# A four-layer block, a hybrid mixer and an expert gather on one core: first-tile rows in ticks of their own, modulation pieces on TensorE, ring loads behind them

## What is computed

```
cond = silu(c)
for i in range(4):                                   # gla, sgu, fox, gla
    shift, scale, gate = split(cond @ w_mod[i] + b_mod[i], 3)
    h = rms_norm(x, norm_pre_g[i]) * (1 + scale) + shift
    x = x + gate * rms_norm(mixer_i(h), norm_post_g[i])
x = x + hybrid_mixer(rms_norm(x, norm_mix))
u = rms_norm(x, norm_ffn)                            # expert layer
# per token 8 heads x 16 picks = 128 picks out of 16384 experts, by top-k over two key sets
a   = gelu(einsum('cd,ced->ce', u, expert_down[idx]))
x   = x + einsum('ce,ced->cd', softmax(best) * a, expert_up[idx])
out = rms_norm(x, final_norm)
```

## Time and profile before

| quantity | value |
|---|---|
| median of 3 runs (lowest, highest) | 1791.57 us (1786.73, 1792.23) |
| the profiled execution's own time | 1788.6 us |
| its span | 1786.8 us |
| PE busy | 1415.5 us, 79% of the span |
| DVE busy | 1034.1 us, 58% |
| ACT, POOL busy | 439.6 us, 489.7 us |
| moved by DMA | 591.53 MB, 331 GB/s over the span |
| mean granted TensorE clock | 0.897 of full |

### The profile page before, as it was taken

The page is one execution under the profiler, slowest core; times in us unless marked ns, Lnnn a source line. Parts: engine busy times, 40 slices in busy tenths (PEclk is TensorE's granted clock), DMA queues, the critical chain, the costliest instruction groups (busy, mean ns, idle before and its releaser), DMA issues. The chain is left out here.

```text
span 1786.8 us, 13852 instructions
## 1 busy us (share of the span) xinstructions
PE 1415.5 (79%) x4134; PEld 714.8 (40%) x4134; DVE 1034.1 (58%) x2185; ACT 439.6 (25%) x993; POOL 489.7 (27%) x498
## 2 busy tenths in 40 slices
PE   2998978798989999996968667698588676776665
PEld 2444445354444554443534333455233322222222
DVE  6654553653132223116587974997963467887875
ACT  2122313425224321011433131231012212211112
POOL 2101100210000000004236435554452354544441
PEclk8998998989999999998978779698799878888888
DMA  9978985976747777879879979999999699999995
GB/s 387 394 248 307 349 307 189 370 280 220 260 171 277 251 264 256 317 261 346 326 281 395 403 239 409 365 415 415 395 410 381 226 418 402 405 422 421 422 421 218
DMA packets 108941, 591.53 MB, mean 331 GB/s; under 512 B 12450, under 2 KB 12706, under 8 KB 60612
## 3 DMA queue, kind: packets, MB, share of 16 engines
q0 software_dynamic: 67776, 312.56, 44.7%
q1 hardware_dynamic: 41092, 278.10, 41.5%
HBM read 589.55 MB, written 1.05 MB: 331 GB/s over the span
## 5 line engine op out<-in xcount | busy, mean ns | idle before, releaser
L928 PE MATMUL bank<-ring,hT 128*128 128x512 f32 x1888 | 867.6, 615 | 44.1 <-DVE room L2009 12.0
L928 PEld LDWEIGHTS bank<-ring,hT 128*128 128x128 f32 x1888 | 366.2, 198 | 488.2 <-issue 451.1
L1168 PE MATMUL bank<-room 128*128 128x512 f32 x360 | 202.0, 713 | 90.2 <-ACT room L1458 74.6
L1757 DVE CUSTOM_DVE_ANT_0 room<-room 128x1024 f32<-128x1024 f32 x172 | 209.1, 1221 | 93.5 <-DMA room<-in_pair,idx 56.0
L859 POOL DMA_INDIRECT room<-in_peer_down,idx x84 | 91.9, 1094 | 514.8 <-DVE idx L1741 402.1
L1168 PEld LDWEIGHTS bank<-room 128*128 128x128 f32 x360 | 78.0, 228 | 211.1 <-ACT room L1458 110.4
L1772 DVE SCALAR_TENSOR_TENSOR x<-room,pcoef,x 128x1024 f32<-128x1024 f32 x113 | 145.3, 1286 | 27.0 <-DMA room<-in_peer_up,idx 23.6
L859 POOL DMA_INDIRECT room<-in_peer_up,idx x115 | 123.4, 1073 | 133.1 <-PE bank L1168 49.7
L907 PE MATMUL bank<-cst,room 128*128 128x128 f32 x424 | 65.7, 300 | 91.5 <-DVE room L1500 43.0
L859 POOL DMA_INDIRECT room<-in_pair,idx x88 | 100.9, 1147 | 111.6 <-PE bank L1168 51.7
L831 POOL DMA_DIRECT2D room<-in_w_mod x80 | 42.3, 530 | 318.1 <-DVE room L1527 199.8
(11 more groups left out here) (298 smaller groups left out, 1456.5 us busy)
## 6 DMA issues: line engine op xcount, KB each, us to landing
ring<-in_wpk SPq DMA_DIRECT2D x248, 1024.0 KB
room<-in_w_mod POOLq DMA_DIRECT2D x80, 512.0 KB
room<-in_w_mod SPq DMA_DIRECT2D x8, 1024.0 KB, 22.9
room<-in_norm_post_g POOLq DMA_DIRECT2D x4, 512.0 KB, 4.8
rowb<-in_gate_bias SPq DMA_DIRECT2D x4, 512.0 KB
room<-in_peer_up,idx POOLq DMA_INDIRECT x115
room<-in_pair,idx POOLq DMA_INDIRECT x88, 12.8
room<-in_peer_down,idx POOLq DMA_INDIRECT x84
```

Of the source, the lines that this page charges most:

```text
L928: last = mm(bank[p][:, :], lhs, ring[:, h % 4, k * N:(k + 1) * N], start=(kk == 0), stop=(h == halves[-1] and k == 3))
L1168: last = mm(bank[WORK[tile][i]][:, :], diag[:, nth % 4, :], row[:, i * N:(i + 1) * N], start=(v == mine[0]), stop=(v == mine[-1]), skip_gr ...
L1757: v.tensor_tensor_reduce(out=row, in0=row, in1=u_(k // MINE), scale=1.0, scalar=0.0, op0=ALU.mult, op1=ALU.add, accum_out=pa[:, k // TOPK ...
```

## The change

- The first tile's last 18 `up` rows get 18 ticks of their own (`REST`): ticks 128 to 145 issue only an `up` row, and pair g belongs to tick g+18. There are 18 ticks more. POOL no longer waits for head 8 before these rows. The rows may use all places, and the pairs take their places in a fixed round that starts with the fifth place in `room` and the four in `ring`; the places 0 to 3 also wait for the last row of a row place whose semaphore they share.
- `on_vector` gives DVE rows 96 to 111 as well, each odd row of 112 to 127, and each odd one of the last eight rows (248 to 255).
- `spot` counts rows instead of ticks against its limit, so it can place six ticks where a tick is one row.
- Of the first 16 modulation pieces, 5, 7, 9, 11, 13 and 15 are not added by DVE. PE multiplies each directly: eight matmuls with a moving side of one column (`piece_columns`), two pieces ahead of everything else and four right before `mod_cols` of layer 0, whose matmuls add to the same columns.
- The first four ring loads also wait for the sixth early load. POOL's first four fetches wait for the ten pieces that DVE still adds (before: for four). DVE's first piece waits for one bias load instead of three.
- ACT loads the table of exp and ln at `final` before it waits for the sums.

```
@@ -229,50 +229,66 @@
-TICKS = PICKS + LEAD[1]
+REST = LEAD[0]
+TICKS = PICKS + REST + LEAD[1]
...
+PE_PIECES = (5, 7, 9, 11, 13, 15)
+
+
+def summed_before(n):
+    return n - sum(i < n for i in PE_PIECES)
...
 def on_vector(u):
-    return u < 6 * TOPK or u % 4 == 3
+    return u < 7 * TOPK or u % 4 == 3 or (u % 2 and (u < MINE or u >= PICKS - 8))
+
+def tick_of(g):
+    return g if g < MINE else g + REST
+
+
+def pick_of(k):
+    g = k if k < MINE else k - REST
+    return None if MINE <= k < MINE + REST or g >= PICKS else g
...
 def added_at(v):
-    return v + LEAD[v // MINE]
-
-
-BORN = [0] * 9 + [9, 9] + [20, 20]
-PAIR, PAIR_LAST = {}, {}
-_last = {}
-for _g in range(MINE, PICKS):
-    _free = [p for p in range(len(BORN)) if _g - MINE >= BORN[p]]
-    _p = min(_free, key=lambda p: _last.get(p, p - 100))
-    PAIR[_g] = (_p, sum(PAIR[g][0] == _p for g in PAIR))
-    if _p in _last:
-        PAIR_LAST[_g] = _last[_p]
-    _last[_p] = _g
+    return tick_of(v) + LEAD[v // MINE]
+
+
+PLACES = (4, 5, 6, 7, 8, 0, 1, 2, 3, 9, 10, 11, 12)
+PAIR = {g: (PLACES[(g - MINE) % len(PLACES)], (g - MINE) // len(PLACES)) for g in range(MINE, PICKS)}
+PAIR_LAST = {g: g - len(PLACES) for g in range(MINE + len(PLACES), PICKS)}
...
-GROUP_AT = {g + n: i for i, (g, n) in enumerate(GROUPS)}
+GROUP_AT = {tick_of(g + n - 1) + 1: i for i, (g, n) in enumerate(GROUPS)}
@@ -396,10 +412,9 @@
     def spot(most):
         rows.add_due()
-        for _ in range(most):
-            target = start + (stop - start) * gone // whole
-            if asked(rows.at) < target:
-                rows.tick()
+        target, most = start + (stop - start) * gone // whole, asked(rows.at) + 2 * most
+        while asked(rows.at) < min(target, most):
+            rows.tick()
@@ -447,13 +462,12 @@
-for _k in range(MINE + LEAD[0]):
+for _k in range(MINE + REST):
...
-        _free = [s for s in PREFER if BORN_AT.get(s, 0) <= _k and not (s in ROWB and _k >= ROWB_ENDS)
-                 and (_k < MINE - 4 or 4 <= s < 8)]
-        _s = min(_free, key=lambda s: (SLOT_LAST[s][0], PREFER.index(s)) if s in SLOT_LAST else (-1, PREFER.index(s)))
+        _s = min((s for s in PREFER if BORN_AT.get(s, 0) <= _k and not (s in ROWB and _k >= ROWB_ENDS)),
+                 key=lambda s: (SLOT_LAST[s][0] if s in SLOT_LAST else BORN_AT.get(s, 0) - 1, PREFER.index(s)))
@@ -698,6 +712,9 @@
+        def sums_set(L):
+            return 48 * (L // 2 + 1) - (0 if L % 2 else 16)
@@ -808,6 +825,7 @@
                         else:
                             sp.wait_ge(S(early_in(h)), 16)
+                            sp.wait_ge(S(early_in(5)), 16)
                         load(ring[:, h % 4, :], A["wpk"][first + i], f"w_in{h % 4}")
@@ -826,7 +844,7 @@
             def fetch(n):
                 L, third, k = PIECES[n]
-                pool.wait_ge(S("summed"), 4 if n < 2 * KC + 4 else n - 3)
+                pool.wait_ge(S("summed"), summed_before(2 * KC if n < 2 * KC + 4 else n - 3))
@@ -837,7 +855,7 @@
                     pool.dma_start(sums[L % 2][i][0:1, :], A["b_mod"][L:L + 1, i * D:(i + 1) * D]) \
-                        .then_inc(S(f"sums_init{L % 2}"), 16)
+                        .then_inc(S("shift_init" if L == i == 0 else f"sums_init{L % 2}"), 16)
@@ -862,10 +880,10 @@
             for step in ORDER:
                 if step[0] == "tick":
-                    g, v = step[1], step[1] - LEAD[0]
-                    if g % TOPK == 0 and g < PICKS:
+                    g = pick_of(step[1])
+                    if g is not None and g % TOPK == 0:
                         pool.wait_ge(S("picked"), g // TOPK + 1)
-                    for kind, r in (("dn", g), ("up", v)):
+                    for kind, r in (("dn", step[1]), ("up", step[1] - LEAD[0])):
                         if not 0 <= r < MINE:
                             continue
                         i, _ = ROW[kind, r]
...
-                    if MINE <= g < PICKS:
+                    if g is not None and g >= MINE:
                         p, nth = PAIR[g]
                         if g in PAIR_LAST:
                             up_used(pool, PAIR_LAST[g])
                         elif p < 5:
                             pool.wait_ge(S("scm1"), 4)
+                            if p < 4:
+                                row_used(pool, SLOT_LAST[8 + p][1])
                         elif p < 9:
                             n, b = use("mm", 1, "query", 3)
                             pool.wait_ge(S(f"pd{b}"), n // 2 + 1)
@@ -957,9 +977,21 @@
...
+            def piece_columns(n, p):
+                _, third, k = PIECES[n]
+                pe.wait_ge(S(early_in(n // 2)), 16)
+                for j in range(KC):
+                    mm(bank[p][:, third * KC + j:third * KC + j + 1], early[n // 2][:, n % 2, j * P:(j + 1) * P],
+                       const("cond", k, 1), start=n == PE_PIECES[0] and j == 0, stop=False, skip_group_check=True)
...
             pe.wait_ge(S("first_in"), 16)
             pe.wait_ge(S("ones_set"), 1)
             pe.wait_ge(S("pool_order"), 1)
+            pe.wait_ge(S("cond"), 1)
+            for piece in PE_PIECES[:2]:
+                piece_columns(piece, use("mod_cols", 0)[1])
@@ -968,19 +1000,22 @@
-                    pe.wait_ge(S(f"sums_init{L % 2}"), 48 * (L // 2 + 1))
+                    if L == 0:
+                        for piece in PE_PIECES[2:]:
+                            piece_columns(piece, p)
+                    pe.wait_ge(S(f"sums_init{L % 2}"), sums_set(L))
                     for j in range(2 * KC):
                         if j % KC == 0:
-                            pe.wait_ge(S("summed"), L * 3 * KC + j + KC)
+                            pe.wait_ge(S("summed"), summed_before(L * 3 * KC + j + KC))
                         last = mm(bank[p][:, j:j + 1], sums[L % 2][j // KC][:, (j % KC) * P:(j % KC + 1) * P],
-                                  ones[:, 0:1], start=True, stop=True)
+                                  ones[:, 0:1], start=L > 0, stop=True, skip_group_check=L == 0)
@@ -1458,6 +1493,7 @@
                 elif kind == "final":
+                    nc.scalar.preload_act_table_set(EXP_SET)
                     act.wait_ge(S(f"out{t}"), 1)
@@ -1511,12 +1547,16 @@
             def add_piece(n):
                 L, third, k = PIECES[n]
-                if n % (3 * KC) == 0:
-                    dve.wait_ge(S(f"sums_init{L % 2}"), 48 * (L // 2 + 1))
+                if n in PE_PIECES:
+                    return
+                if n == 0:
+                    dve.wait_ge(S("shift_init"), 16)
+                elif n % (3 * KC) == 0 or n == KC:
+                    dve.wait_ge(S(f"sums_init{L % 2}"), sums_set(L))
                 if n == 0:
                     dve.wait_ge(S("cond"), 1)
                 else:
-                    dve.wait_ge(S("summed"), n)
+                    dve.wait_ge(S("summed"), summed_before(n))
@@ -1751,12 +1791,13 @@
             def tick(k):
-                if k < PICKS:
-                    row, landed, count = landed_row("dn", k)
+                g = pick_of(k)
+                if g is not None:
+                    row, landed, count = landed_row("dn", g)
                     dve.wait_ge(landed, count)
...
-                hh, e = k // TOPK, k % TOPK
+                if g is None:
+                    return
+                hh, e = g // TOPK, g % TOPK
                 if hh + 1 < T * PH and hh + 1 != PH and e in (2, 4, 6, 8):
                     choose(hh + 1, e // 2 - 1)
```

More of the change, by code:

```diff
@@ L259 @@
 DVE_NTH = {u: i for i, u in enumerate(ON_DVE)}
+ADDS = {added_at(v): [v] for v in range(PICKS)}
 def adds_of(k):
-    return [v for v in (k - LEAD[0], k - LEAD[1]) if 0 <= v < PICKS and added_at(v) == k]
+    return ADDS.get(k, [])
 def sums_at(hh):
-    return (hh + 1) * TOPK if hh < PH else MINE + 1 if hh == PH else (hh - 1) * TOPK + 6
+    return (hh + 1) * TOPK if hh < PH else MINE + 1 if hh == PH else (hh - 1) * TOPK + REST + 6
 EXP_NTH = {hh: i for i, hh in enumerate(sorted(range(T * PH), key=lambda hh: (sums_at(hh), hh)))}
@@ L322, in tick @@
             self.add_through(v - 4)
-        self.add_through(PAIR_LAST.get(self.at))
+        self.add_through(PAIR_LAST.get(pick_of(self.at)))
         for v in adds_of(self.at):
@@ L326, in tick @@
                 self.add_through(ON_PE[PE_NTH[v] - 4])
-        if self.at == MINE + BORN[-1]:
+        if self.at == tick_of(MINE + 9):
             self.add_through(MINE - 1)
@@ L425, in make_order @@
         rows.add_due()
-        if rows.at == MINE + LEAD[0] + 8:
+        if rows.at == tick_of(MINE + 8):
             rows.add_through(MINE - 1)
@@ L1233, in _ @@
                         if L == 3 and t == 0 and i == 0:
-                            act.wait_ge(S("summed"), len(PIECES))
+                            act.wait_ge(S("summed"), summed_before(len(PIECES)))
                         if L == 3 and t == 0 and i == 2:
@@ L1449, in _ @@
                         w, e = g // TOPK % 4, g % TOPK
```

(11 more changed lines are left out.)

2 lines of the change are left out of this document (1 added, 1 removed).

## The result

| | before | changed |
|---|---|---|
| median of the runs | 1791.9 us (4 runs, 1786.7 to 1792.3) | 1745.1 us (4 runs, 1739.4 to 1747.6) |
| profiled execution | 1788.6 us, span 1786.8 | 1739.4 us, span 1737.6 |
| ratio, with 95% interval | | 0.9739 (0.9714 to 0.9765) |

The change is 46.8 us faster; the forecast had 27, and its range ended at 1749. The prediction was right on the sign and wrong on the size.

The account below looks back on a forecast made before the run. DMA was taken as full except a hole at 1360 to 1415 us, a late start and the tail. From 1788.6: -24 + 0 + 2 - 5 = -27, 1761.6; 3.0 more for the median, 1764.5 us; range 1749 to 1783.

Parts of the forecast that it names:

- Part 1: DMA hole at 1360 to 1415 us: own ticks for rows and 16 more rows on DVE fill it; 24 us gained.
- The bound: Saturated DMA from 1360 us on: 158.0 MB at 0.421 MB/us takes 375 us, it took 405; at most 30 gained.
- the ten rows that were to go out during the picking: While DVE picks head 8, ten rows can still go out: 5.2 MB or 12.5 us of transfers.
- (b): Rival: the hole is filled by half because POOL waits for DVE; 12 us instead of 24, 1776.5; chance 0.15.
- Part 2: Ticks three earlier move up to six rows from 1150 to 1360 into 820 to 1150 us; 0 us.
- Part 3: Start: loads arrive earlier, but modulation columns on PE end at 43.6, 3.5 us late; 2 us lost in all.
- (a): Rival: the clock stays full through the columns, start 2 us gained instead of 2 lost; 1760.5; chance 0.10.
- Part 4: Tail: last rows split anew save 2.4 us, one early table load replacing two saves 2.6; 5 us gained.
- (c): Rival: the earlier ticks lengthen 820 to 1150 us, 7 us lost; 1771.5; chance 0.07.
- (d): Rival: rows in their own ticks become a serial chain, first pair at 1451; slower, 1796; chance 0.04.
- (e): Rival: POOL waits for the scores anyway and the hole only moves; 1788.6; chance 0.04.
- the signs the forecast named: Hole's DMA share 0.9 or more, POOL's PE waits gone, columns done at 43 to 44, one end table load, 17 us tail.

Follow-up runs that it names:

- e10: The changed kernel with both the old rule for ticks and the old preference for row places; 1770.1 us, ratio 0.9894.
- T: The change's new rule for where a tick may go, which puts ticks earlier; alone on the kernel before it measured 1782.1 us.
- P: The change's new preference for row places: a place just come into being waits behind places free for longer; alone on the kernel before 1778.2 us.
- e2: The kernel before with only the new rule for where a tick may go; 1782.1 us, ratio 0.9940.
- e15: The kernel before with only the new preference for row places; 1778.2 us, ratio 0.9928.
- e11: The kernel before with the new rule for ticks and the new preference for row places, nothing else; 1767.1 us, ratio 0.9870.
- e12: The changed kernel run once more, word for word, in a later set; 1742.2 us, ratio 0.9741.
- e6: The changed kernel without the table load ahead of the last normalization; 1750.5 us, ratio 0.9766.
- e9: The changed kernel with ticks moved earlier still, by two (three at the third layer's first blocks); 1752.0 us, ratio 0.9788.
- e7: The changed kernel with three of the first sixteen modulation pieces on PE (5, 7 and 9) instead of six; 1738.6 us, ratio 0.9718.

## Why the prediction was right or wrong

**Part 1, the hole, 24 us: right in mechanism, too large.** e10 is the change without T and P, so it has just the parts that the forecast gave a price other than 0. It gained 19 us where the sum said 27. Its stretches:
```profile
1360.00:1415.00 55.00, 37.04 (x117) 18.93 (x115) 40.14 (x77) 12.79 (x26) 28.11 (x26) 0.84 0.92 357
1415.00:1530.00 115.00, 63.59 (x118) 24.16 (x117) 90.82 (x222) 24.44 (x57) 52.78 (x49) 0.85 1.01 414
```
Over rows 2 that is 5.9 and 1.8 MB more, 7.7 MB, 18 us at 0.421 MB/us. By the time it is 19 less the tail's 4.5, and 1 or 2 more for the start, 15 to 17. So part 1 was worth 15 to 18. Three things were off. The bound took 0.421 MB/us for the hole as well, but at 0.92 of full share the hole moves 357 GB/s, which makes 388 at full share. And the picking of head 8 was put at 1379.5 to 1388.6, behind PE. In e10 PE's last query block ends at 1384.34 (forecast 1386), and ACT has the scores of head 8 ready at 1378.2. But DVE works on three `dn` and three `up` rows without a gap from 1377.87 and comes to the picking only at 1385.52. And the ten rows that were to go out during the picking did not: POOL issues one more at 1386.72 and then waits 8.88 us, the DMA share from 1390 to 1400 is 0.60, and the first pair goes out at 1420.77 and not at 1411. That is part of rival (b).

**Part 2, the ticks three earlier, 0 us: wrong. Here the forecast failed, and in the term that it did not have (next paragraph).** The forecast said that "both stretches pay in the same coin", because DVE is about as busy in each. DVE's share of busy time was the wrong thing to compare. In 820 to 1150 us the DMA share was 0.91 with dips under 0.6, and in the stretch behind it 1.0. A MB moved from the full stretch into a dip was gained, with DVE as busy as it was. The upper bound of 7.5 us was near: 11 us (7 to 14, by the interval of e2) in the kernel before.

**The preference for row places: not in the forecast at all.** It stands in the diff as the key of a `min`, and its price stood in the trace, 11.96 and 19.64 us of POOL's waiting. It is worth 13 us by itself (10 to 16, by the interval of e15). With part 2 this is the whole of what was missing: 23 us (e11), less the 8 by which the rest was set too high, and some 5 more when everything is together (47 - 19 - 23), which the intervals hardly separate from 0.

**Part 3, the start, 2 us lost: near for the columns, its cost at the end not shown.** The forecast gave 43.6 for the modulation columns, between 37.9 and 45.5; they ended at 45.97 in the profiled change, just outside, and at 42.82 in e12. Of PE's lateness at the first projection (5.9 us) 2.4 us were left at 84 us, and the bytes are 2.5 us behind at 87 us, 1.0 in e12 (389 GB/s). Further on it can't be followed. POOL's first gather of a row, at the end of tile 0's chain, is at 815.13 before and 821.25 in the change, but at 820.29 in e2 and 821.87 in e11, which have the old start. No run takes the whole start back. How many pieces PE takes makes no difference that the runs can show. The 2.30 us that the forecast took for a group at full clock are not the least: at the second layer's columns the first group took 1.84 us (144.04, before) with the clock at 1.00. Rival (a) did not come: in e12 the granted clock falls to half while PE is busy without a gap with one-column matmuls.
```profile
26.00:32.00 6.00, 6.00 (x44) 6.00 (x45) 2.57 (x2) 0.00 (x0) 1.25 (x3) 0.81 1.04 428
32.00:39.00 7.00, 7.00 (x34) 7.00 (x35) 0.00 (x0) 0.00 (x0) 0.85 (x2) 0.50 0.99 408
```
The Trainium skill ("TensorE: Matmul & The Clock Gate", section "What's actually happening") has the gate go by how busy PE has been. These rows have a PE that is busy all of the time by the profile, and a clock at half. So the trace sides against the plain reading of that sentence, as the forecast took it. Whether the chip counts one-column matmuls as busy is not shown.

**Part 4, the tail, 5 us: right.** 1.9 for the rows (forecast 2.4) and 2.56 for the loads (2.6), 4.5 together. From the last row used to the end of the span it was 19.4 us before (from 1767.38) and is 14.9 now. The Trainium skill ("ScalarE: Activation LUTs", section "What ACT_TABLE_LOAD costs") gives about 2.66 us a switch, which would be an estimated 5.3 for both; e6 against the change shows 2.56 for both.

**The rivals.** (a) is answered above. (b), the hole filled by half, came in part: 15 to 18 us instead of 24, where (b) had 12. (c), that earlier ticks lengthen 820 to 1150, is wrong for this step; a further one does lose time (e9, 8 us). (d), the serial chain, needed a first pair later than 1447; it was at 1394.89, and POOL sent a row every 1.3 us. (e) is out: PE's wait left POOL. Of the signs the forecast named, the share of 0.93 in the hole, POOL's waits for PE, the one table load and the tail of about 17 us came as said. The columns missed the 43 to 44, and the part of the gain that was missing stood in a stretch that it had named no sign for.

## What to carry to other kernels

Where transfers set the end, list the waits of the engine that issues them, stretch by stretch, and give every dip of the DMA share a name before pricing an edit: each rule in a diff that decides which buffer the next gather takes belongs to one of those waits. A free buffer is not the same as one that will be free soon. With an issuer that works in order, taking the second while others lie free stops everything behind it, here for 12 and 20 us. Moving transfers from a full stretch to one with dips can be a gain although the other engines are as busy in both on average. It has an end: two ticks further lost 8 us.

## What the runs showed of the chip that was not expected

At the start of the program the clock column can't be taken at its word. In the change the table gives 1.00 for every stretch up to 46 us, while 16 records of one-column matmuls (one group) take 3.4 us (13.65 for 64). That is the time that they take where 0.50 is shown (3.57 at 31.94 in e7). In e12 the same 64 took 10.55 us, with the clock shown as falling to 0.50 between 26 and 32 us. At full clock a group took 1.93 us (27.08 in e7), and 1.84 us at 144.04 in the kernel before, where the column shows 1.00 in the middle of the program. So the two executions of one kernel differ by 3.1 us at the start, and the times show which clock PE had where the clock column does not.
